# Gate multiplied in the output stage, half of two tiles' output product made in the last inverse, w_out split by ScalarE and VectorE

## The reference, cut to what matters

```python
y_h = _hyena_branch(hy_streams, conv_w, conv_b, k_freq, hyena_bias)
y_p = _pool_branch(pool_in, pool_w, pool_scale)
y = concatenate([y_h * silu(hy_gate), y_p * silu(pool_gate)], axis=-1)
out = gate[:, None, :] * (y @ w_out + b_out)
h = _layer_norm(DEEPNORM_ALPHA * h + out, ln_g, ln_b)
```

## Time and profile before

| | |
|---|---|
| median of 3 runs | 1316.59 us |
| profiled execution, own time | 1325.41 us |
| its span | 1323.6 us |
| PE busy in the span | 1124.8 us (85%) |
| DVE, ACT, POOL busy | 862.2, 557.3, 59.5 us |
| last inverse, from its first load to the end of its last operation | 1054.0 to 1128.96 us |
| first load of the output stage | 1129.87 us |
| last product ended, normalisation of the last tile begins | 1313.49 us |

### The profile page before, as it was taken

One profiled execution on the slowest core, in us unless ns is written; L12 is line 12 of the kernel. 1 busy time (PEld: TensorE's weight loads), 2 busy tenths in 40 slices (PEclk: granted clock), 3 DMA queues, 4 the chain that ended last, 5 costly groups with the idle time before them and its releaser, 6 DMA issues. The chain is left out here.

```text
span 1323.6 us, 14489 instructions
## 1 busy us (share of the span) xinstructions
PE 1124.8 (85%) x4940; PEld 859.1 (65%) x4940; DVE 862.2 (65%) x1092; ACT 557.3 (42%) x745; POOL 59.5 (4%) x50
## 2 busy tenths in 40 slices
PE   3778827899999999979899887999888546899996
PEld 1356615688887877757677765666666334688885
DVE  5868839655554364539888545538779448577776
ACT  2437735343343333427666424325676445211110
POOL 0010013100000000000000000000000014000000
PEclk9779958899999999999999989999999869899999
DMA  8359989577754235578898578758988598622221
GB/s 299 117 171 351 311 234 320 194 244 253 262 181 167 80 98 190 192 198 236 237 268 239 155 208 262 235 195 231 262 256 231 174 361 275 238 96 96 95 95 48
DMA packets 156176, 276.48 MB, mean 209 GB/s; under 512 B 24711, under 2 KB 46215, under 8 KB 153994
## 3 DMA queue, kind: packets, MB, share of 16 engines
q1 hardware_dynamic: 151613, 269.53, 64.4%
q0 software_dynamic: 3168, 5.51, 1.5%
q10 hardware_dynamic: 1328, 0.59, 0.2%
HBM read 183.30 MB, written 98.57 MB: 213 GB/s over the span
## 5 line engine op out<-in xcount | busy, mean ns | idle before, releaser
L150 PE MATMUL prj_pp<-prj_uhi,prj_whi 128*128 128x512 f32 x768 | 309.3, 403 | 8.1 <-PEq L222 4.2
L151 PE MATMUL prj_pp<-prj_ulo,prj_whi 128*128 128x512 f32 x768 | 304.9, 397 | 0.0
L152 PE MATMUL prj_pp<-prj_uhi,prj_wlo 128*128 128x512 f32 x768 | 304.7, 397 | 0.0
L150 PEld LDWEIGHTS prj_pp<-prj_uhi,prj_whi 128*128 128x128 f32 x768 | 147.6, 192 | 50.7 <-issue 19.1
L152 PEld LDWEIGHTS prj_pp<-prj_uhi,prj_wlo 128*128 128x128 f32 x768 | 147.1, 191 | 32.3
L151 PEld LDWEIGHTS prj_pp<-prj_ulo,prj_whi 128*128 128x128 f32 x768 | 147.6, 192 | 31.0
L150 PE MATMUL out_ps<-whl,out_yhi 128*128 128x512 f32 x256 | 102.3, 400 | 4.3 <-DVE out_ylo L2008 4.3
L152 PE MATMUL out_ps<-whl,out_ylo 128*128 128x512 f32 x256 | 102.1, 399 | 0.0
L151 PE MATMUL out_ps<-whl,out_yhi 128*128 128x512 f32 x256 | 102.1, 399 | 0.0
L1180 DVE TENSOR_TENSOR p_alo<-p_a,p_ahi 128x1024 fp32r<-128x1024 f32 x32 | 39.1, 1223 | 71.4 <-ACT p_ahi L1108 71.4
L1108 ACT ACTIVATE p_ahi<-p_a 128x1024 fp32r<-128x1024 f32 x32 | 33.9, 1059 | 116.8 <-PE p_ps L152 104.0
(11 more groups left out here) (183 smaller groups left out, 2031.8 us busy)
## 6 DMA issues: line engine op xcount, KB each, us to landing
kseq<-fs_xo SPq DMA_DIRECT2D x32, 512.0 KB, 5.7
p_a<-kseq SPq DMA_DIRECT2D x32, 512.0 KB, 4.4
kfreq<-p_out SPq DMA_DIRECT2D x32, 512.0 KB, 5.2
xseq<-p_xo SPq DMA_DIRECT2D x32, 512.0 KB, 6.8
p_a<-xseq SPq DMA_DIRECT2D x32, 512.0 KB, 6.7
p_k_re<-kfreq SPq DMA_DIRECT2D x64, 256.0 KB, 4.4
p_k_im<-kfreq SPq DMA_DIRECT2D x64, 256.0 KB, 5.3
bseq<-p_out SPq DMA_DIRECT2D x32, 512.0 KB, 6.0
```

The costliest lines, as they stand in the source:

```text
L150: nc.tensor.matmul(out, w[0], m[0], start=start, stop=False, skip_group_check=True)
L151: nc.tensor.matmul(out, w[0], m[1], start=False, stop=False, skip_group_check=True)
L152: return nc.tensor.matmul(out, w[1], m[0], start=False, stop=stop, skip_group_check=True)
```

## The change

The Hyena gate is no longer loaded and multiplied in the last inverse. ACT copies the transposed bank into `za` there, and the output stage loads the gate in four 1 MB pieces (`gb`) and multiplies on DVE, tile by tile, before it splits. Buffers that both stages use now live in a class `Mix`. During the last inverse the first 1 MB piece of the pooled half is loaded and split for two tiles, and PE makes the pooled half of the product (24 of 48 matmuls) of tile 0 in step 12 and of tile 1 in step 16; the output stage begins with the Hyena halves of these two. POOL no longer takes part: DVE makes the low part of `w_out`. The lists of ACT and DVE in the last inverse, and SP's in both stages, are written in a new order. The loops of the output stage are unrolled.

```diff
@@ Mix: used by both stages
+    def load_pooled(self, sp, yp, c):
+        if c >= 2:
+            sp.wait_ge(self.plo_done[1], 2 * (c - 2) + 2)
+        cols = slice(c * CH, (c + 1) * CH)
+        sp.dma_start(self.yb[c % 2][:, :, :], yp[:, :, cols].rearrange("k p t -> p k t")).then_inc(self.yb_in[c % 2], 16)
+    def pooled_high(self, act, n):
...
+    def product(self, n, ks, start, stop):
+        r = n % 2
+        for h in range(2):
+            cols = slice(h * CH, (h + 1) * CH)
+            for k in ks:
+                mm = mm3(self.nc, self.ps[r][:, h, :], (self.yhi[r][:, k, :], self.ylo[r][:, k, :]),
+                         (self.whl[:, 0, k, cols], self.whl[:, 1, k, cols]), start and k == ks[0], stop and k == ks[-1])
@@ last_inverse, SP
-            for n in range(4):
-                load(n)
+            load(0)
+            load(1)
             load_w(0)
+            load(2)
             load_w(1)
-            for k in range(4):
-                sp.dma_start(ya[:, k, :], g2[k, :, :]).then_inc(ya_in, 16)
+            load(3)
             for n in range(4, GS):
                 load(n)
+                if n == 5:
+                    mix.load_pooled(sp, yp, 0)
                 if n % 2 == 1:
                     load_w(n // 2)
@@ last_inverse, PE
-            staggered(GS, (inv, 0), (turn, 2))
+            for step in range(S):
+                if step < GS:
+                    inv(step)
+                if step == 12 or step == 16:
+                    n = (step - 12) // 4
+                    for b in range(2):
+                        pe.wait_ge(wlo_done[b], 2)
+                    pe.wait_ge(mix.plo_done[n], 1)
+                    mix.product(n, range(4, KT), True, False)
+                if 0 <= step - 1 < GS:
+                    turn(step - 1)
@@ last_inverse, ACT
-            staggered(GS, (evac, 2), (high, 0), (whigh, 2))
+            for step in range(S):
+                if step < GS:
+                    high(step)
+                if 0 <= step - 1 < GS:
+                    evac(step - 1)
+                if 0 <= step - 2 < GS:
+                    turned(step - 2)
+                if step in split_at:
+                    w_high(split_at[step])
+                if step == 8 or step == 10:
+                    mix.pooled_high(act, (step - 8) // 2)
@@ last_inverse, DVE
-            staggered(GS, (low, 0), (wscale, 1), (gated, 3))
+            for step in range(S):
+                if step < GS:
+                    low(step)
...
+                if step in split_at:
+                    w_scale(split_at[step])
+                if step - 1 in split_at:
+                    w_low(split_at[step - 1])
+                if step == 9 or step == 11:
+                    mix.pooled_low(dve, (step - 9) // 2)
@@ output_norm, SP
-            load_yb(0)
-            pipeline(sp, GS, [(load, 0), (store, 2)])
+            load_gate(0)
+            load(0)
+            sp.dma_start(ln_g[:, :], t["ln_g"][0, :].partition_broadcast(P)).then_inc(consts, 16)
+            sp.dma_start(ln_b[:, :], t["ln_b"][0, :].partition_broadcast(P)).then_inc(consts, 16)
+            mix.load_pooled(sp, yp, 1)
+            load_gate(1)
+            for n in range(1, GS + 2):
...
@@ output_norm, PE
+            for n in range(GS):
+                r = n % 2
+                if n >= 2:
+                    pe.wait_ge(mix.plo_done[r], n // 2 + 1)
+                    pe.wait_ge(mix.sum_done[r], n // 2)
+                    mix.product(n, range(4, KT), True, False)
+                pe.wait_ge(clo_done[r], n // 2 + 1)
+                mix.product(n, range(0, 4), False, True).then_inc(mix.mm_done[r], 1)
@@ output_norm, DVE
-            pipeline(dve, GS, [(low, 0), (skip, 0), (norm, 1)])
+            for n in range(GS + 1):
+                if n < GS:
+                    gate(n)
+                    if n >= 2:
+                        mix.pooled_low(dve, n)
+                    conv_low(n)
+                    skip(n)
+                if n >= 1:
+                    norm(n - 1)
```

More of the change, by code:

```diff
@@ L1778, in last_inverse @@
+def last_inverse(nc, t, tabs, bseq, rows, g2, yp, mix):
     with Scope(nc, "fin") as s:
@@ L1909, in output_norm @@
+def output_norm(nc, t, g2, yp, mix, out):
     with Scope(nc, "out") as s:
-        yb = s.sb("yb", [P, 4, L])
-        yhi = [s.sb(f"yhi{b}", [P, KT, P], F32R) for b in range(2)]
-        ylo = [s.sb(f"ylo{b}", [P, KT, P], F32R) for b in range(2)]
+        yg = [s.sb(f"yg{b}", [P, 4, P]) for b in range(2)]
         x = [s.sb(f"x{b}", [P, D]) for b in range(2)]
@@ L1931, in _, with load_gate @@
         def _(sp):
[L1932 removed]
+            def load_gate(c):
+                if c >= 2:
+                    sp.wait_ge(gated[1], 2 * (c - 2) + 2)
                 cols = slice(c * CH, (c + 1) * CH)
[L1934 to L1946 removed]
@@ new lines, in load, with store @@
+            def load(n):
+                r = n % 2
+                after(sp, skip_done[r], n // 2)
+                sp.dma_start(x[r][:, :], t["x"][0, P * n:P * n + P, :]).then_inc(x_in[r], 16)
+            def store(n):
+                r = n % 2
+                sp.wait_ge(o_done[r], n // 2 + 1)
+                sp.dma_start(out[0, P * n:P * n + P, :], o[r][:, :]).then_inc(stored[r], 16)
+            load_gate(0)
+            load(0)
+            sp.dma_start(ln_g[:, :], t["ln_g"][0, :].partition_broadcast(P)).then_inc(consts, 16)
@@ new lines, in _, with conv_high, root @@
+        @block.scalar
+        def _(act):
+            def conv_high(n):
+                r = n % 2
+                act.wait_ge(gated[r], n // 2 + 1)
+                after(act, mix.mm_done[r], n // 2)
+                nc.scalar.activation(mix.yhi[r][:, 0:4, :], yg[r][:, :, :], ACT.Copy).then_inc(chi_done[r], 1)
+            def root(n):
+                r = n % 2
+                act.wait_ge(var_done[r], n // 2 + 1)
+                nc.scalar.activation(sm[r][:, 0:1], mv[r][:, 1:2], ACT.Sqrt, bias=eps[:, 0:1]).then_inc(root_done[r], 1)
+            act.wait_ge(eps_set, 1)
+            for n in range(GS + 1):
+                if n < GS:
+                    if n >= 2:
+                        mix.pooled_high(act, n)
+                    conv_high(n)
+                if n >= 1:
+                    root(n - 1)
@@ L2014, in skip, with gate @@
-            def skip(it, b):
-                r, used = at(it, b, 2)
-                dve.wait_ge(x_in[r], 16 * used + 16)
-                after(dve, o_done[r], used)
-                nc.vector.scalar_tensor_tensor(out=res[r][:, :], in0=x[r][:, :], scalar=ALPHA, in1=gate_bias[:, :],
-                                               op0=ALU.mult, op1=ALU.add).then_inc(skip_done[r], 1)
-            def norm(it, b):
-                r, used = at(it, b, 2)
-                STEPS = 6
-                n = STEPS * used
-                done = [0]
+            def gate(n):
+                r, c = n % 2, n // 4
+                dve.wait_ge(mix.gb_in[c % 2], 16 * (c // 2) + 16)
+                after(dve, clo_done[r], n // 2)
+                nc.vector.tensor_tensor(yg[r][:, :, :], mix.za[:, :, P * n:P * n + P], mix.tokens(mix.gb, n),
+                                        ALU.mult).then_inc(gated[r], 1)
@@ L2027, in then, with norm @@
+            def norm(n):
+                r, used = n % 2, n // 2
+                STEPS = 5
+                done = [STEPS * used]
                 def then(ins):
-                    ins.then_inc(step[r], 1)
+                    ins.then_inc(step_done[r], 1)
                     done[0] += 1
-                    dve.wait_ge(step[r], n + done[0])
+                    dve.wait_ge(step_done[r], done[0])
                 dve.wait_ge(skip_done[r], used + 1)
-                dve.wait_ge(mm_done[r], used + 1)
```

225 lines of the change are left out of this document (103 added, 122 removed).

## The result

The changed kernel takes 1320.44 us (median of 13 runs, 1316.81 to 1329.03), the kernel before 1316.0 on the same chip (13 runs, 1311.31 to 1320.18); the ratio is 1.0036, with a 95% interval of 1.002 to 1.0053. The forecast was 1320.1, slower. The total is right; two terms of the sum are off by 4 us each, and they cancel.

The account below looks back on a forecast made before the run. The output stage was taken as PE-bound, the last inverse as bound by no single engine. Last inverse +3.8, output stage -2.0, clock +1.2, scope +0.5 give +3.5 us: 1316.6 + 3.5 = 1320.1 us, range 1311 to 1327.

Parts of the forecast that it names:

- The sign and its mechanism: Whole kernel: slower by 3.5 us, with the last inverse 3.8 us longer as the early products are largely exposed.
- Wait for block 2: Last inverse: w_out's second block lands at 1079.2, the scaling wants it at 1077.8, so 1.4 us are lost.
- The pair of steps: Last inverse: two steps take 6.7 us (6.5 to 6.95), with ACT waiting for DVE rather than transfers binding.
- the fall of the clock: Rival, chance 0.14: PE falls to half clock in the last inverse's gaps, 1.0 us in each of five pairs; 1327 us.
- The sign given ahead: Profile after, last inverse: high to high of even steps is 6.5 to 7 us, ACT waiting for DVE's scaling in each.
- two further pairs: Last inverse: these and the pooled split of two tiles lead from high(6) at 1083.7 to step 12 at 1105.4.
- The strided copy: Last inverse: ACT's copy into za takes a slot of 0.49 to 0.96 us, taken as 0.72.
- the bound: Last inverse: za's copy at either end of its range moves the stage by 1.7 us each way.
- the rival of short waits: Chance 0.18: block 2 in time, strided copy as cheap as plain, no clock fall, no scope cost; 1315.3 us.
- The clock after the gap before tile 2: Output stage: after PE's 4.0 us gap, half of a 2.4 us half-clock loss is counted, +1.2 us (0 to 2.4).
- The output matmuls at 0.233 us: Output stage: each matmul keeps its earlier duration, 11.2 us for the 48 of a tile, fourteen tiles after tile 1.
- DVE and the added transfers in later tiles: Output stage: DVE's list fills 9.4 of 11.2 us per tile and 4 MB of gate meets free DMA; both cost nothing.

Follow-up runs that it names:

- experiment 5: Kernel after without the two early products, whose pooled halves are multiplied at the start of the output stage; 0.9957 of the kernel before.
- experiment 8: Kernel after with ACT's copy into za written without the stride, leaving out the reordering of tokens; 1.0039 of the kernel before.
- experiment 2: Kernel after with pads so that whl alone begins 32 bytes off a multiple of 64; 1.0082 of the kernel before.
- experiment 12: Kernel after with ACT's even-step copy of w_out ahead of the two copies that wait for PE; 1.0083 of the kernel before.
- experiment 9: Kernel before with whl on a multiple of 64 bytes and three more pads aligning operands of earlier stages; 0.9932 of the kernel before.

## Why the prediction was right, and where it was wrong

- **The sign and its mechanism: right.** The early products are exposed (predicted 4.2 us of tile 0 and all 5.6 of tile 1; measured 4.1 and 5.0 by experiment 5, against which the kernel after is 0.8% slower), the output stage starts at E+7.27 (7.3), x of tile 1 is taken up at E+16.0 (16.1) and tile 2 at E+24.73 (24.9). Wait for block 2: 1.79 (1.4). POOL's 30.6 us of SP's waits were exchanged for 33.9 on PE.
- **The pair of steps: right as a floor, too low as a mean.** 6.74 against 6.7. Failed is the step that gave the fall of the clock a rival's place instead of a place in the sum. Three pairs had a whole product at half clock; it cost 1.24 us in two of them, and 0.54 in the third on top of DVE's pooled low part: 2 x 1.24 + 0.54 = 3.0 us. 0.6 more is the pooled low part of tile 1, which the sum left out (7.88 = 6.74 + 0.60 + 0.54), and 0.4 block 2. That is 4.0, and F to E is off by 3.8. The sign given ahead, that high to high of even steps would be 6.5 to 7 us with ACT waiting for DVE's scaling in each, did not come: from step 2 to step 12 they took 7.3 to 8.8, and in the pairs at half clock ACT waited for PE, not for the scaling. The rival had the price of a slow pair nearly right (1.0, measured 1.24), and it came in three pairs, not in five; the product of tile 0 ran at full clock. In the trace after, the two products that began after 4.56 and 4.21 us of idle time ran at half clock, those after 1.43 and 1.21 did not, and the one after 2.85 began at full clock and fell before it ended. The Trainium skill, page "TensorE: Matmul & The Clock Gate", Part 1, says that idleness throttles the array; this trace agrees. But the idle time just before a product does not settle it: the one after 2.07 us ran at half clock and the one after 2.34 at full. (The text of that step says "two further pairs"; its number holds three.)
- **The strided copy: dear, but hidden.** It took 1.07 us against 0.60 for the plain one, and where nothing else holds ACT its next instruction starts 0.84 to 0.89 us after that copy's start, in the upper half of the range of 0.49 to 0.96. The Trainium skill, page "SBUF — State Buffer", section "Door 1: The DMA port swizzle", says that an access that crosses to a new line of 16 bytes pays a penalty; experiment 8 agrees, 1.07 against 0.59. But what the copy delays, the even high part, is wanted by DVE only at 3.38 us after the odd one, and is done at 3.35: the path through DVE's list is as long. So the sum led the pair through ACT's copy where DVE's list decides. With the copy as it is the two paths tie at 6.74, and with a plain copy the pair stays at that, where the bound and the rival of short waits took 1.7 us off the stage. Experiment 8 shows it.
- **The clock after the gap before tile 2: right.** The first six matmuls ran at full clock, then eight stood 0.43 apart, 1.6 us lost, for which the sum had 1.2. In experiment 2, after 3.51 us of idle time, tile 2 began at half clock, so the term could as well have been the full 2.4.
- **The output matmuls at 0.233 us: wrong, by 4.5 us.** 14 tiles of 48 at 0.2267 are 152.3 us, not 156.8. This is the term that made the total come out. The duration was a row of before, and the operand that it was read from is one that the change moved. The second experiment has the kernel without that gift: the last product's end at E+184.3, ratio 1.0082.
- **DVE and the added transfers in later tiles: nothing**, as predicted; PE has no third gap.

So that the forecast of 1320.1 met 1320.4 is luck: the mechanism of the early products is right, and two errors of 4 us cancel. With the 4.0 us of the last inverse in the sum, and 0.233 us for a matmul as it had, it would have been 1324; at equal addresses the runs show some 11 us more than before, about 1327.

## What to carry to other kernels

Find the loop of a stage that waits, by its round: from one instruction to its next instance, through every engine's list; only what stands on that round counts, and what is moved behind its last wait counts in full in every round that this path sets (experiment 12), however idle the engines are. Work that is to fill an idle engine belongs where that engine waits for something from outside, here behind the stage boundary (experiment 5). And a duration read from the trace goes with its operand's address: if a change moves a tile, look where it lands.

## What the runs showed of the hardware

- **The address of the operand sets the pace of a matmul.** 128x512 fp32r matmuls whose streamed operand begins 32 bytes past a multiple of 64 in each partition started 0.2333 us apart in the output stage, on a multiple of 64 0.2267; both ways in both kernels. The same shift of the streamed operand gave 0.001 us in the spectrum products (experiment 9). Why more there than elsewhere stays open; it was not tried whether another distance matters, or whether it is the place of the other operand against this one.
- **An ACT copy from PSUM that writes at a stride of 64 bytes** took 1.07 us where the plain one took 0.59 (128x512, f32). Whether it is the stride or the further dimension of the pattern was not separated.
- **Six matmuls more in most even steps** raised the mean granted clock from 0.80 to 0.90 in one stretch of 17 us and from 0.85 to 1.00 in the next of 18.5, and still left the first products of two pairs at half clock (1.2 in place of 2.4 GHz).
- **The same idle time, three clocks.** The product of step 9 begins after 2.85 us of idle time in the kernel after and in experiments 2 and 8. In the kernel after it falls to half within itself, in experiment 2 it runs at half (0.69, then 0.63), in experiment 8 it stays at full (0.50, then 0.39). The pair took 7.82, 8.41 and 7.82 us.
